# A hybrid S5, latent-attention and expert-retrieval block on one core: squares of x partly summed by GpSimd, normalization set among the weight rows, and tile 0's turn, query and top-k ahead of tile 1's second projection half

## The reference

```python
mod = (jax.nn.silu(c) @ w_ada + b_ada)[:, None, :]
shift_m, scale_m, gate_m, shift_f, scale_f, gate_f = jnp.split(mod, N_ADA, axis=-1)
h = rms_norm(x, norm_mix) * (1.0 + scale_m) + shift_m
proj = h @ w_in
...
y = jnp.concatenate([rms_norm(y_ssm, out_norm_ssm), rms_norm(y_attn, out_norm_attn)], axis=-1) @ w_out
x = x + gate_m * y
h2 = rms_norm(x, norm_ffn) * (1.0 + scale_f) + shift_f
return x + gate_f * peer_ffn(h2, w_query, sub_keys, expert_down, expert_up)
```

## Time and profile before

| | us |
|---|---|
| median of 3 runs | 3250.51 |
| lowest and highest | 3246.43, 3251.78 |
| span of the profiled execution, first to last instruction | 3247.0 |

### The profile page before, as it was taken

The page is one execution under the profiler, slowest core; times in us unless marked ns, Lnnn a source line. Parts: engine busy times, 40 slices in busy tenths (PEclk is TensorE's granted clock), DMA queues, the critical chain, the costliest instruction groups (busy, mean ns, idle before and its releaser), DMA issues.

```text
span 3247.0 us, 38518 instructions
## 1 busy us (share of the span) xinstructions
PE 2362.8 (73%) x13186; PEld 1943.1 (60%) x13186; DVE 2206.0 (68%) x5266; ACT 2035.2 (63%) x3762; POOL 1321.2 (41%) x1190
## 2 busy tenths in 40 slices
PE   5977787777778797676676677766767667776766
PEld 4654456666666565565665566665666566665655
DVE  6881547767778576677666666666666666666654
ACT  3313416767777566676666766676667766766665
POOL 1140313323434344444445454444444444544543
PEclk9988998988878798777767776777677777767766
DMA  6600039988888999999999999999999999999997
GB/s 250 189 14 4 34 146 419 386 320 322 345 335 346 418 419 420 420 421 421 421 422 420 418 421 419 419 411 420 421 419 413 419 417 418 415 417 419 418 420 326
DMA packets 175461, 1162.57 MB, mean 358 GB/s; under 512 B 22720, under 2 KB 23632, under 8 KB 43808
## 3 DMA queue, kind: packets, MB, share of 16 engines
q0 software_dynamic: 148352, 1077.61, 81.0%
q1 hardware_dynamic: 25680, 78.30, 6.5%
q10 hardware_dynamic: 1232, 4.20, 0.3%
HBM read 1147.32 MB, written 11.53 MB: 357 GB/s over the span
## 4 chain that ended last, share of the span: by engine, by line
DMA 33%; DVE 23%; PE 16%; ACT 11%; issue 4%; POOL 1%; POOLq 0%; DVEq 0%; SPq 0%
DMA pair<-in_experts_dram,idx_g 32%; DVE pair L1693 11%; PE acc_a L1357 5%; ACT pair L1492 5%; PE pef L1332 3%; PE acc_b L1357 2%; ACT L1488 2%; PE acc_b L1237 1%; ACT w L1490 1%; PE pef L1256 1%; ACT pex L1433 1%; DVE top_i L1621 1%; DVE staged L1622 1%; ACT ga L1488 1%; DVE top_i L1624 1%
## 5 line engine op out<-in xcount | busy, mean ns | idle before, releaser
L1192 POOL DMA_INDIRECT pair<-in_experts_dram,idx_g x1024 | 1215.8, 1187 | 1484.1 <-PE acc_a L1357 865.1
L1693 DVE SCALAR_TENSOR_TENSOR pair<-pair,h 128x1024 f32<-128x1024 f32 x1024 | 1247.3, 1221 | 666.2 <-DMA pair<-in_experts_dram,idx_g 664.7
L1357 PE MATMUL acc_a<-ident,pair 128*128 128x128 f32 x5120 | 878.7, 333 | 443.2 <-ACT pair L1492 435.4
L1492 ACT ACTIVATE pair<-pair,w 128x1024 f32<-128x1024 f32 x1024 | 1176.2, 1149 | 33.3
L1357 PEld LDWEIGHTS acc_a<-ident,pair 128*128 128x128 f32 x5120 | 738.1, 173 | 576.3 <-ACT pair L1492 546.0
L1357 PE MATMUL acc_b<-ident,pair 128*128 128x128 f32 x3072 | 592.6, 361 | 292.9 <-ACT pair L1492 292.4
L1357 PEld LDWEIGHTS acc_b<-ident,pair 128*128 128x128 f32 x3072 | 488.6, 187 | 391.4 <-ACT pair L1492 386.7
L1488 ACT ACTIVATE ga<-a 128x1 f32<-128x1 f32 x1024 | 204.1, 199 | 687.3 <-DVE pair L1693 682.5
L1490 ACT ACTIVATE w<-ga,g 128x1 f32<-128x1 f32 x1024 | 301.6, 295 | 33.2
L1332 PE MATMUL pef<-h2t,wq 128*128 128x128 f32 x1536 | 196.6, 291 | 1.6 <-DMA wq<-in_w_query_t_dram 1.6
L1332 PEld LDWEIGHTS pef<-h2t,wq 128*128 128x128 f32 x1536 | 195.0, 209 | 2.8 <-issue 2.8
(11 more groups left out here) (341 smaller groups left out, 2365.6 us busy)
## 6 DMA issues: line engine op xcount, KB each, us to landing
wada<-in_w_ada_t_dram SPq DMA_DIRECT2D x48, 512.0 KB, 5.8
pair<-in_experts_dram,idx_g POOLq DMA_INDIRECT x1024, 16.2
pieces<-in_w_query_t_dram SPq DMA_DIRECT2D x16, 512.0 KB, 8.2
wq<-in_w_query_t_dram SPq DMA_DIRECT2D x4, 2048.0 KB, 35.9
ht<-in_x_t_dram ACTq DMA_DIRECT2D x4, 1024.0 KB, 15.1
wout_a<-in_w_out_dram SPq DMA_DIRECT2D x1, 4096.0 KB, 13.1
x2s<-out_dram SPq DMA_DIRECT2D x8, 512.0 KB, 12.3
out_dram<-h SPq DMA_DIRECT2D x8, 512.0 KB, 8.9
```

Of the source, the lines that this page charges most:

```text
L1192: p.indirect_dma_start(pair[n % R], None, A["experts"], bass.IndirectOffsetOnAxis(ap=idx[:, t % (2 * PH), k:k + 1], axis=0)).then_inc(pair ...
L1357: last = t.matmul(accs[ACC[i]][:, k * P:(k + 1) * P], pair[n % R][:, D + k * P:D + (k + 1) * P], S.ident[:], is_transpose=True, start=n % ...
L1492: s_.activation(pair[n % R][:, D:], pair[n % R][:, D:], ACT.Copy, scale=w[:, n % NA:n % NA + 1]).then_inc(scaled, 1)
L1693: v.scalar_tensor_tensor(down, down, 1.0, h2[:, n // P, :], ALU.mult, ALU.mult, accum_out=a[:, n % NA:n % NA + 1]).then_inc(dotted, 1)
```

## The change

Three things are changed.

1. **Squares.** A new SBUF tensor `late_squares` holds the squares of k = 4 to 7, so only k = 2 and 3 wait for `sq_used`. GpSimd adds the four into the first of them with three dependent additions of 128 x 1024, each as soon as the next square is there. TensorE sums five tensors over the channels in place of eight. The additions stand in GpSimd's queue between the loads of `win_m` and `win_s`.
2. **Normalization.** VectorE waits for the broadcast `rb` after row 9 in place of after row 15. It then normalizes one group after each of rows 9 to 15, and the last behind them.
3. **Order at the join.** On TensorE, turn(0), queries(0) and scores(0) stand ahead of project_att(1). On ScalarE, scored(0) and softened(0) stand ahead of square(1). On VectorE, the top-k of task 0 and weigh_less(0) stand ahead of combine(1), add_x(1), make_h2(1) and shift_h2(1).

```diff
+    late = place(nc, "late_squares", [P, 4, SEQ], 58)
...
@@ gpsimd, phase_ab
             pool.dma_start(win_m[:], w[:, :, DS:]).then_inc(wm_in, 16)
+            for k in range(1, 4):
+                pool.wait_ge(sq_ready, 4 + k + 1)
+                nc.gpsimd.tensor_tensor(late[:, 0], late[:, 0], late[:, k], ALU.add).then_inc(late_summed, 1)
+                pool.wait_ge(late_summed, k)
             pool.wait_ge(w_used, EARLY)
...
@@ scalar, phase_ab
             for k in range(KD):
                 act.wait_ge(x_in[k // 2], 16)
-                if k >= 2:
+                if k in (2, 3):
                     act.wait_ge(sq_used, k - 1)
-                s.activation(sqx[:, k % 2], ht[:, k], ACT.Square).then_inc(sq_ready, 1)
-            act.wait_ge(sq_used, KD)
+                s.activation(sqx[:, k % 2] if k < 4 else late[:, k - 4], ht[:, k], ACT.Square).then_inc(sq_ready, 1)
+            act.wait_ge(sq_used, 5)
...
@@ tensor, phase_ab
-            for k in range(KD):
-                pe.wait_ge(sq_ready, k + 1)
+            for k in range(5):
+                if k < 4:
+                    pe.wait_ge(sq_ready, k + 1)
+                else:
+                    pe.wait_ge(late_summed, 3)
...
@@ vector, phase_ab
+            def normalize(k):
+                v.tensor_tensor(ht[:, k], ht[:, k], rb[:], ALU.mult).then_inc(xn_ready, 1)
+
             for b in range(8, EARLY):
                 weigh_row(b)
-            dve.wait_ge(row_done, 1)
-            for k in range(KD):
-                v.tensor_tensor(ht[:, k], ht[:, k], rb[:], ALU.mult).then_inc(xn_ready, 1)
+                if b == 9:
+                    dve.wait_ge(row_done, 1)
+                if b >= 9:
+                    normalize(b - 9)
+            normalize(KD - 1)
...
@@ tensor, phase_ef
             project_ssm(1)
-            project_att(1)
             turn(0)
             queries(0)
             scores(0)
+            project_att(1)
             turn(1)
...
@@ scalar, phase_ef
             queried(0)
+            scored(0)
+            softened(0)
             square(1)
-            scored(0)
             turned(1)
-            softened(0)
...
@@ vector, phase_ef
             shift_h2(0)
+            for m in range(PARTS):
+                find_part(0, m)
+            own.wait()
+            weigh_less(0)
             combine(1)
             add_x(1)
             make_h2(1)
             shift_h2(1)
-            for m in range(PARTS):
-                find_part(0, m)
-            own.wait()
-            weigh_less(0)
             weigh(0)
```

More of the change, by code:

```diff
@@ L181, in phase_ab @@
         silu_ready, dt_ready, angles_ready, trig_ready, mag_ready = (sem(f"a_{n}") for n in ("silu", "dt", "angles", "trig", "mag"))
-        sq_ready, sq_used, std_ready, rstd_ready, row_done, xn_ready, mod_ready = (sem(f"a_{n}") for n in ("sq", "squsd", "std", "rstd", "row", "xn", "mod"))
+        sq_ready, sq_used, late_summed, std_ready, rstd_ready, row_done, xn_ready, mod_ready = (sem(f"a_{n}") for n in ("sq", "squsd", "late", "std", "rstd", "row", "xn", "mod"))
         ha_ready, hd_ready = sem("a_ha"), sem("a_hd")
@@ L319, in _ @@
             pe.wait_ge(zeroed, 3)
-            for k in range(KD):
-                pe.wait_ge(sq_ready, k + 1)
+            for k in range(5):
[3 more added lines that the diff above has]
+                    pe.wait_ge(late_summed, 3)
                 for i in range(NT):
-                    last = t.matmul(k0[:, i:i + 1], sqx[:, k % 2, tile(i)], ones[:, 0:1], start=k == 0 and i == 0, stop=k == KD - 1,
-                                    skip_group_check=True)
+                    last = t.matmul(k0[:, i:i + 1], sqx[:, k % 2, tile(i)] if k < 4 else late[:, 0, tile(i)], ones[:, 0:1],
+                                    start=k == 0 and i == 0, stop=k == 4, skip_group_check=True)
                 last.then_inc(sq_used, 1)
```

## The result

The changed kernel takes **3257.95 us** (median; 3256.09 to 3259.19), the kernel before 3248.42 us on the same chip: ratio 1.0033, 95% interval 1.0021 to 1.0044, **9.5 us slower**. The forecast was 3259. The profiled span is 3255.6 us against 3247.0, so 8.6 us longer.

What follows compares the result with a forecast made beforehand. VectorE, ScalarE and TensorE bound the middle stretch, gathers the last. Join 11.7 less start 3 gave +8.7 us on span 3247.0, so 3255.7, plus 3.5 to the median: 3259 us; range 3245 to 3266, forecast's own 3256 to 3264.

Steps and rivals of the forecast that it cites:

- The bound: From 520 to 1100 us VectorE, ScalarE and TensorE set the pace; delays at first slots come out at the end.
- The start: Squares and normalization: adds end at 35.8, broadcast at 43.7, norms at 60.2 against 62.9; gain 2.7 us, taken as 3.
- The join: Tile 0 goes first; tile 1's queries and `pieces` come later, group 2 ends 13.2 to 16.2 us late.
- The 8.2 us of VectorE's order: At the join, combine(1) waits behind task 0's top-k, so h2 of tile 1 is ready 8.2 us later.
- The slack of 3.0: Group 3's scores, staged at 513.7, are taken up by VectorE at 516.7; 3.0 us of delay is absorbed.
- the middle that I took, 11.7: VectorE is 10.2 to 13.2 us late at slot 10; the middle, 11.7 us, was taken as the join's cost.
- The step from span to time: Whole run: the median of the runs, 3250.51, is 3.5 above the profiled span, turning 3255.7 into 3259 us.
- (a): Join: `pieces` land in 3.3 us or delay is partly absorbed; +2, 3252.6 us; chance 0.25 together with (c).
- (b): Join: the gathers' start counts, 4.2 us sooner, carried by nine buffers; faster, 3242 us; chance 0.14.
- (c): Join: gathers are the limit but dry up between 502 and about 512; +3 net, 3253.5 us; 0.25 with (a).
- (d): Join: the reordering does nothing because turn(0) still waits for tile 1; excluded by the order, no chance given.
- (e): Start: adds conflict more, no gain left, with 13.2 at the join; 3264 us; 0.58 together with the forecast.

Runs made afterwards that it cites:

- e2_join: Kernel before with only the reordering at the join, its start as before: 3259.46 us, ratio 1.0037 to before.
- e8_vector_old: Changed kernel with VectorE's old join order and ScalarE's square(1) and turned(1) ahead of softened(0), TensorE's new order kept: 3250.42 us, ratio 1.0010 to before.
- e11_best_again: Kernel before plus the new squares without interleaved normalization, and ScalarE's square(1) ahead of queried(0); a repeat run: 3239.53 us, ratio 0.9974 to before.
- the first run of the late exponentials: Kernel before plus new squares, early square(1), and ScalarE's queried(1) and scored(1) ahead of softened(0): 3236.02 us, ratio 0.9969 to before.
- e10_normal: Kernel before with only the normalizations placed among the weight rows, squares summed as before: 3246.49 us, ratio 0.9994 to before.
- e4_held: Changed kernel with GpSimd's first gather held until TensorE finishes tile 1's query group 1: 3254.12 us, ratio 1.0021 to before.
- e5_root_late: Changed kernel with GpSimd's root for tile 1 moved behind its first three gathers: 3257.89 us, ratio 1.0035 to before.
- e12_exp_again: Kernel before plus new squares, early square(1), and ScalarE's queried(1) and scored(1) ahead of softened(0); repeat run: 3239.21 us, ratio 0.9969 to before.

## Why the prediction came out right

- **The bound.** That what VectorE, ScalarE and TensorE lose at the first slots comes out at the end undiminished was the base of the sum, and it held: slot 11 is 9.5 us late, the last slot 8.7, the median 9.5. Over the experiments slot 11 and the median move together (+11.7 and +12.2 in e2_join, +3.3 and +3.3 in e8_vector_old, -8.3 and -8.2 in e11_best_again), within about 3 us, but for the first run of the late exponentials (-7.0 and -12.7) and for e10_normal (+2.4 and -2.2), which both gained about 3 to 5 us more on the kernel before between 738 and 778 us.
- **The start.** Broadcast at 42.6 where I had 43.7 (35.8 for the adds was too dear: they ended at 34.5), norms done at 58.6 and not 60.2. But the projection started 3.5 us sooner, where these alone would have given 4.3: the scalings beside the fill, which I had called mostly covered, took back 0.8. Two errors of opposite sign, 1.6 us and 0.8, around the 2.7 that the sum gave and the 3 that I took.
- **The join.** turn(0) at 447.48 (forecast 447), first gather at 472.51 (472), turn(1) at 474.90 (475), `pieces` 8.10 us (8.1), tenth gather at 510.67 (509), slot 11 at 528.84 (528). The first GELU at 506.09 is 1.8 us behind the sum (507.3 less 3). The 8.2 us of VectorE's order is the measured term to a tenth. The step that rested on the earlier trace rows, that the next load would take as long as a load among gathers had taken, is what e4_held bears out.
- **Mis-sized.** Query group 1 I took at its old 5.54; it was 6.58. Group 2 ended 16.3 us late, just beyond my 13.2 to 16.2 and 1.6 over their middle. The slack of 3.0 was right: the scores of group 3 were staged 15.6 us late (again from combine(0)) and taken up 12.7 late. What offset the 1.6 were two terms that I didn't have, 0.7 us between group 2 and those scores and 0.4 at slot 11, where the kernel before had waited 0.35 for a gather. So the middle that I took, 11.7, came within 0.6 of the 12.3 measured in part by luck.
- **The time itself.** Sum and spans agree closely: +8.7 against +8.6, and 3255.7 us against 3255.6. The step from span to time doesn't hold. I added 3.5 us, the distance from the one span to the median of three runs; in the changed kernel's profiled execution it is 1.8 (3257.47 against 3255.6), and over six runs the median before is 3248.42 and not 3250.51. Against that median the loss is 9.5. That 3259 stands so near to 3257.95 is a sum that was 0.8 short on a start that was 2.1 high.
- **Rivals.** (a) had `pieces` at 3.3 us or more of the delay absorbed; they took 8.10, and 12.3 of 16.3 us came through. (b), the gathers' start, is refuted twice over by e4_held and e5_root_late. (c) needed the gathers to be the limit: so they are only once the query path is shortened, as in e12_exp_again. (d) fell with turn(0), which ran at 447.48. (e) fell with the adds: they ended 1.3 us sooner than I had counted.

About the page on the lock (the Trainium skill, SBUF — State Buffer, "Who interferes with whom"), from which I took the end 35.8. The instructions of the tile `late_squares` (ns, min/median/max):

```profile
L233 POOL TENSOR_TENSOR late_squares<-late_squares x3: 2352/3202/3203, 25.6 to 31.3; 128x1024 f32<-128x1024 f32 x3
```

and VectorE's rows of `wada` beside them:

```profile
27.52 1.52 DVE L409 SCALAR_TENSOR_TENSOR wada<-wada,silu_c 128x1024 f32<-128x1024 f32 x1 [5.87 <-DMA wada<-in_w_ada_t_dram]
...
30.57 1.74 DVE L409 SCALAR_TENSOR_TENSOR wada<-wada,silu_c 128x1024 f32<-128x1024 f32 x1 [1.53 <-DMA wada<-in_w_ada_t_dram]
...
33.63 1.97 DVE L409 SCALAR_TENSOR_TENSOR wada<-wada,silu_c 128x1024 f32<-128x1024 f32 x1 [1.30 <-DMA wada<-in_w_ada_t_dram]
```

The adds lose 2 x 0.85 = 1.7 us and the rows, 1.22 alone, lose 0.30 + 0.52 + 0.75 = 1.6: together 3.3, near the 3 x 1.22 = 3.7 that began beside adds. So the trace agrees with mutual exclusion in the main; what I had wrong was to charge all of it to the adds. The same section says that VectorE's tensor_scalar can use both pairs of ports, and that whichever of it and a GpSimd instruction is issued first then shuts the other out. The fill agrees: it began first, took its usual 3.53 us up to 61.40, and the three TENSOR_SCALAR begun at 58.94 ended 2.0 us behind it, where they take 2.26 alone. Of a VectorE instruction outside those modes with at most one input in SBUF the section says that it doesn't contend with GpSimd. The normalizations are such, since `rb` lies in PSUM, and the 9.13 us beside the fill agree. What the fill would do beside a TENSOR_TENSOR with both inputs in SBUF no run here shows.

## What to carry to other kernels

Getting one tile's work done early was worth nothing here, where it only filled buffers, and cost what it delayed the next tile's chain; follow each early transfer to what it will stand in front of. A load that took 3 us with no gather ahead of it took 8 behind a burst of them, so put the small load that gates the next matrix work ahead of the burst. Look at what an instruction comes to stand beside, and not only at when it starts: the same fill was free beside multiplications with an input in PSUM and nearly doubled the scalings.

## What the runs showed that I had not expected

- TensorE seems to pay for standing still twice, though no run varied the idle time alone: query group 1 took 3.84 us at a granted clock of 1.00 (e11_best_again, directly behind other products), 5.54 at 0.68 (before) and 6.58 at 0.56 (e4_held, where TensorE had stood for 11.7 us before turn(1)). Group 2 ran from 7.14 to 10.16 us. From the kernel before to the changed one, the delay on VectorE so grew by 3.3 us on TensorE.
- A wait can cost less than no wait: holding the gathers back for 14 us made the kernel 3.8 us faster.
- With squares and early square in place, two chains (gathers for slots 0 to 9, queries for group 2) nearly tie: with the second 3 us shorter, slot 11 came 73.5 us after combine(0) instead of 73.2, and the medians are 3239.2 and 3239.5.
- What stays open: why executions part by up to 6 us between 738 and 778 us, behind everything that was edited. It is as much as anything here is worth. The granted clock there differs between executions, but it doesn't go with the gain in every pair, and its cause was not tried.
